# Attention stage of a two-layer trunk: one 384-column projection per unit from dense token copies

## The chip, the cores and the metric

The kernel runs on one core of one Trainium2 chip. The time is device microseconds of one execution; the kernel before took 3385.18 us (median of three runs, 3384.01 to 3385.2). TensorE (PE) multiplies, VectorE (DVE), ScalarE (ACT) and GpSimd (POOL) work element by element, and SyncE's queue (SP) issues DMAs. PEld is TensorE's weight load, which overlaps its matmuls.

## The reference

One sequence of 1024 tokens with 1024 channels goes through two layers. Layer 0 mixes tokens by attention, layer 1 by an mLSTM; each is followed by a squared-ReLU MLP. Only the attention is touched by the change:

```python
qkv = (x @ w_in).reshape(b, s, 3, N_GROUPS, ATTN_HEADS, ATTN_HEAD_DIM)   # 3 groups, 16 heads of 64
for g, (window, dilation) in enumerate(((128, 1), (512, 4), (2048, 16))):
    q = rms_norm(qkv[:, :, 0, g], q_gain[g]) * (ATTN_HEAD_DIM ** -0.5)
    k = rms_norm(qkv[:, :, 1, g], k_gain[g])
    o, l = dilated_window_attention(q, k, qkv[:, :, 2, g], rel_bias[:, g], window, dilation)
wts = softmax(stack(lses), axis=0)             # the three groups are merged by their denominators
y = einsum('gbsh,gbshe->bshe', wts, stack(outs))
x = x + y @ w_out
```

A query at token t sees the tokens t, t-d, ..., t-window of its group, where d is the group's dilation: 1, 4 or 16.

## The kernel before, in words

Every matrix product is made from two halves of each operand, hi and lo, in three matmuls: hi times hi, hi times lo, lo times hi (`split_matmul`, lines 67 to 71). A product over 1024 channels is thus 24 matmuls, 8 channel tiles by 3.

The attention stage (`attention_phase`) works on 24 sections: 8 pairs of heads by 3 groups, the group being the section number modulo 3. A section has 8 steps j, one for each 128 tokens, and a unit is one block of 128 queries of one section. All engines run the same list of steps (`run_supersteps`), and are held together by semaphores alone, each of them strictly in the order in which its own code is written. T counts the steps (8 times the superstep, plus j).

In step T TensorE does, in this order: query and key of the 128 tokens of step T (24 matmuls of 256 columns into ps_qk, with the tokens as the stationary operand); the transposes of the normed query and key of the step before, and of one block of values (ps_t); the transposes of probabilities (ps_p); a quarter of the values of half of the tokens (6 matmuls of 512 columns into ps_v, the weights stationary, the tokens streamed in their natural order); the scores of one unit (ps_s); and the product of probabilities and values of the unit before it (ps_o). Units run 8 steps behind the projection. A unit whose queries also see the block of keys before it has two blocks of keys (it is called two-block here) and takes twice the transposes and value products: 7 of 8 units in group 0, 4 of 8 in group 1 and none in group 2.

Where the group's dilation is not 1, ScalarE and VectorE reorder tokens after the fact: they read ps_t and ps_v in a strided order (`perm_view`) when they write qk_hi, qk_lo and vT.

ScalarE in step T: exponentials of a unit (L635), the copies of a finished output block out of ps_o (L651, L652), the hi half of the next section's weights (L602), the squares of query and key (L667), and what was transposed in this step (L673, L684, L688). The output copies of step T need the ps_o product of step T-1. VectorE: bias and row maximum of a unit (L723), the sums of squares (L732, L737), the lo halves (L743, L758, L764), the normed query and key (L779), and in some steps a piece of the merge of the three groups (L804 to L847; 1024 columns in the large ones). GpSimd: the lo half of the weights (L857), and a power of four numbers per token, rs (L879).

After the attention stage the projection of its output starts (the first matmul into first_ps), and then come the MLP, the mLSTM and the second MLP, none of which changes.

## Time and profile before

| | |
|---|---|
| median of three runs | 3385.18 us |
| the profiled execution's own time | 3383.74 us |
| its span, first to last instruction | 3382.0 us |
| TensorE busy | 3192.3 us (94%) |
| VectorE, ScalarE, GpSimd busy | 1334.0, 1102.1, 825.2 us |
| granted TensorE clock, mean | 0.978 |

Matmuls are pipelined, so their busy times overlap and the distance from one start to the next is what one costs. The same holds to a lesser degree on ScalarE and VectorE, where an instruction may start about 0.1 us before the one ahead of it has ended. The attention stage fills the first 1333 us of the span.

### The profile page before, as it was taken

What the parts mean: (1) busy time and instruction counts of PE and PEld (TensorE: products, weight loads), DVE (VectorE), ACT (ScalarE), POOL (GpSimd) and SP (SyncE); (2) the same over time, 40 slices, a digit from 0 to 9 for tenths busy, and PEclk for the clock granted to TensorE, in tenths of its full rate; (3) what the DMA queues carried; (4) which work ended last, traced back from release to release, by engine and by line L of the source; (5) the groups of instructions that cost most, each with busy time, mean ns of one, the idle gap of its engine ahead of it and who ended that gap; (6) DMA issues with size and microseconds to landing.
All of it is one profiled execution on the core that took longest, in us unless ns stands there. A gap on an engine that the chain in (4) does not pass through costs nothing. (4 is left out here: it accounts for less than half of the span.)

```text
span 3382.0 us, 48256 instructions
## 1 busy us (share of the span) xinstructions
PE 3192.3 (94%) x17466; PEld 2669.5 (79%) x17466; DVE 1334.0 (39%) x3725; ACT 1102.1 (33%) x3002; POOL 825.2 (24%) x598
## 2 busy tenths in 40 slices
PE   4999999999999995999999999899877999999999
PEld 3888888888888883878888888678655788888887
DVE  6445454555555554341313133541064431313131
ACT  4555555555555553321111112210244211111020
POOL 3332333333233320212222122112111122222221
PEclk9999999999999995999999999999998999999999
DMA  2112121211112114111111111111201111111112
GB/s 98 36 40 59 41 58 40 61 49 50 52 45 53 47 32 150 50 44 47 48 50 44 50 50 45 38 44 50 81 26 57 44 50 44 50 50 44 50 45 80
DMA packets 89904, 177.01 MB, mean 52 GB/s; under 512 B 25515, under 2 KB 55870, under 8 KB 89662
## 3 DMA queue, kind: packets, MB, share of 16 engines
q1 hardware_dynamic: 87358, 169.63, 16.1%
q10 hardware_dynamic: 2304, 4.20, 0.3%
q8 instruction: 147, 2.41, 0.3%
q14 instruction: 95, 0.78, 0.1%
HBM read 160.67 MB, written 13.12 MB: 51 GB/s over the span
## 5 line engine op out<-in xcount | busy, mean ns | idle before, releaser
L69 PE MATMUL ps_qk<-w_hi,attn_hT_hi 128*128 128x256 f32 x1536 | 437.4, 285 | 23.3 <-DVE attn_hT_lo L213 9.7
L915 POOL TENSOR_TENSOR first_w_lo<-first_raw,first_w_hi 128x1024 fp32r<-128x1024 f32 x96 | 231.7, 2414 | 900.8 <-ACT first_w_hi L911 900.8
L70 PE MATMUL ps_qk<-w_lo,attn_hT_hi 128*128 128x256 f32 x1536 | 436.1, 284 | 0.0
L71 PE MATMUL ps_qk<-w_hi,attn_hT_lo 128*128 128x256 f32 x1536 | 436.1, 284 | 0.0
L857 POOL TENSOR_TENSOR w_lo<-raw,w_hi 128x384 fp32r<-128x384 f32 x192 | 194.6, 1015 | 701.9 <-ACT w_hi L602 701.9
L915 POOL TENSOR_TENSOR second_w_lo<-second_raw,second_w_hi 128x1024 fp32r<-128x1024 f32 x72 | 172.2, 2391 | 630.0 <-ACT second_w_hi L911 630.0
L69 PEld LDWEIGHTS ps_qk<-w_hi,attn_hT_hi 128*128 128x128 f32 x1536 | 294.1, 191 | 27.6 <-issue 13.3
L635 ACT ACTIVATE prob<-ps_s,neg_max 128x128 f32<-128x128 f32 (+1 forms) x384 | 156.6, 413 | 439.7 <-DVE neg_max L726 439.7
L70 PEld LDWEIGHTS ps_qk<-w_lo,attn_hT_hi 128*128 128x128 f32 x1536 | 294.7, 192 | 0.4
L71 PEld LDWEIGHTS ps_qk<-w_hi,attn_hT_lo 128*128 128x128 f32 x1536 | 294.9, 192 | 0.0
L69 PE MATMUL first_ps<-first_hid_hi,first_w_hi 128*128 128x512 f32 x640 | 255.4, 399 | 32.7 <-DVE first_hid_lo L1239 32.7
L732 DVE TENSOR_REDUCE ss<-sq 128x4 f32<-128x256 f32 x192 | 80.7, 420 | 506.9 <-ACT sq L667 506.9
L69 PE MATMUL first_ps<-first_hT_hi,first_w_hi 128*128 128x512 f32 x640 | 252.6, 395 | 14.2 <-POOL first_w_lo L915 14.2
L69 PE MATMUL second_ps<-second_hid_hi,second_w_hi 128*128 128x512 f32 x640 | 251.0, 392 | 12.5 <-DVE second_hid_lo L1242 12.5
L70 PE MATMUL first_ps<-first_hid_lo,first_w_hi 128*128 128x512 f32 x640 | 254.9, 398 | 0.0
L71 PE MATMUL first_ps<-first_hid_hi,first_w_lo 128*128 128x512 f32 x640 | 254.7, 398 | 0.0
L70 PE MATMUL first_ps<-first_hT_lo,first_w_hi 128*128 128x512 f32 x640 | 251.4, 393 | 0.0
L71 PE MATMUL first_ps<-first_hT_hi,first_w_lo 128*128 128x512 f32 x640 | 251.4, 393 | 0.0
L70 PE MATMUL second_ps<-second_hid_lo,second_w_hi 128*128 128x512 f32 x640 | 250.5, 391 | 0.0
L71 PE MATMUL second_ps<-second_hid_hi,second_w_lo 128*128 128x512 f32 x640 | 250.1, 391 | 0.0
L879 POOL TENSOR_TENSOR rs<-var,minus_half 128x4 f32<-128x4 f32 x192 | 193.3, 1007 | 133.5 <-DVE var L737 125.0
L911 ACT CAST first_w_hi<-first_raw 128x1024 fp32r<-128x1024 f32 x96 | 99.9, 1041 | 383.6 <-PE first_ps L71 358.5
(276 smaller groups left out, 6853.9 us busy)
## 6 DMA issues: line engine op xcount, KB each, us to landing
raw<-in_wqkv SPq DMA_DIRECT2D x192, 192.0 KB, 2.3
first_raw<-in_w SPq DMA_DIRECT2D x64, 512.0 KB, 3.4
second_raw<-in_w SPq DMA_DIRECT2D x64, 512.0 KB, 3.4
w_bc<-share_dram SPq DMA_DIRECT2D x48, 256.0 KB, 4.2
first_raw<-in_vo_pieces SPq DMA_DIRECT2D x16, 512.0 KB, 3.5
bias<-bias_dram SPq DMA_DIRECT2D x16, 256.0 KB, 3.6
yT_dram<-o_g SPq DMA_DIRECT2D x8, 512.0 KB, 3.1
first_raw<-in_attn_wo SPq DMA_DIRECT2D x8, 512.0 KB, 3.5
```

The source lines that it names most:

```text
L69: pe.matmul(out, a_hi, b_hi, start=first, stop=False)
L70: pe.matmul(out, a_hi, b_lo, start=False, stop=False)
L71: return pe.matmul(out, a_lo, b_hi, start=False, stop=last)
L635: a = act.activation(prob[:, u % 2, h, c0:2 * P], ps_s[h][:, c0:2 * P], ACT.Exp, bias=neg_max[:, sp_, h * TT + u:h * TT + u + 1], accum_ou ...
L732: dve.tensor_reduce(ss[:], sq[:].rearrange("p (h e) -> p h e", e=HD), AX.X, ALU.add)\
L857: pool.tensor_tensor(w_lo[:, par, k, :], raw[:, slot, :], w_hi[:, par, k, :].bitcast(F32), ALU.subtract).then_inc(w_lo_done, 1)
L879: pool.tensor_tensor(rs[:], var[:], minus_half[:], ALU.pow).then_inc(rs_done, 1)
L911: act.copy(self.hi[:, n % 2, :], self.raw[:, n % self.RAW, :]).then_inc(self.hi_done, 1)
L915: pool.tensor_tensor(self.lo[:, n % 2, :], self.raw[:, n % self.RAW, :], self.hi[:, n % 2, :].bitcast(F32), ALU.subtract).then_inc(self.lo ...
```

## The change

The 128 tokens of a step are now the tokens of the unit itself, and not 128 neighbours. For group 1 these are tokens 4 apart, for group 2 tokens 8 apart (every second one of which belongs to another residue of the dilation 16, and is masked by the bias table). Query, key and value of the unit are then one product: 24 matmuls of 384 columns into ps_qkv, the unit's tokens stationary. The 6 matmuls of 512 columns, the tile vT, its copies by ScalarE and its transposes are gone.

For groups 1 and 2 the stationary operand is read from dense copies: ScalarE writes tile_hi, GpSimd writes tile_lo (128 partitions by 1024 columns each, two buffers), one step ahead. Group 0 reads the hidden state directly. In a step of TensorE the product with the values (ps_o) now stands directly behind the projection and works on a unit one step older than before; the scores are last. Units run 2 steps behind the projection, not 8. ScalarE still copies the output out of ps_o for the unit that is two behind its scores. The merge of the groups works on all 128 partitions with 8 columns in place of 64 with 16; its small pieces come one superstep earlier, and its five large ones (1024 columns each, L830 to L847 before) now stand in the steps j = 1, 3, 4, 5 and 6 of a section of group 1. Before, the first stood at j = 7 of such a section and the others at j = 1 to 4 of the next.

```diff
+def tile_view(h, section, u):
+
+    if section % NG == 1:
+        return h[:].rearrange("p k (n i r) -> p k r n i", n=2, r=4)[:, :, u // 2, u % 2, :]
+    return h[:].rearrange("p k (m u) -> p k u m", u=TT)[:, :, u, :]
...
-LAST_SUPER = SECTIONS + 2
+LAST_SUPER = SECTIONS + 1
+LAG = 2
...
-            return TT <= TT * st + j - back < TT * (SECTIONS + 1)
+            return 0 <= TT * st + j - LAG - back < TT * SECTIONS
 
         def unit(st, j, back):
 
-            sec, u = divmod(TT * (st - 1) + j - back, TT)
-            return sec, u
+            return divmod(TT * st + j - LAG - back, TT)
...
+        def next_tile(st, j):
+
+            st, j = (st, j + 1) if j + 1 < TT else (st + 1, 0)
+            return (st, j) if st < SECTIONS and st % NG else None
...
+                def project(k_first, k_end):
+
+                    g = st % NG
+                    for k in range(k_first, k_end):
                         if st == 0 and j % 4 == 0:
                             norm.wait_tile(pe, j // 4, k)
                         if j == 0:
                             pe.wait_ge(w_hi_done, TT * N + k + 1)
                             pe.wait_ge(w_lo_done, TT * N + k + 1)
-                        mm = split_matmul(pe, ps_qk[j % 2][:, 0:2 * P],
-                                          hT_hi[:, k, j * P:(j + 1) * P], hT_lo[:, k, j * P:(j + 1) * P],
-                                          w_hi[:, par, k, 0:2 * P], w_lo[:, par, k, 0:2 * P], k == 0, k == KT - 1)
-                    mm.then_inc(qk_mm, 1)
-                if (st >= 1 or j >= 1) and st <= SECTIONS:
-
+                        h_hi = tile_hi[:, j % 2, k, :] if g else hT_hi[:, k, j * P:(j + 1) * P]
+                        h_lo = tile_lo[:, j % 2, k, :] if g else hT_lo[:, k, j * P:(j + 1) * P]
+                        mm = split_matmul(pe, ps_qkv[j % 2][:, 0:W3], h_hi, h_lo,
+                                          w_hi[:, par, k, :], w_lo[:, par, k, :], k == 0, k == KT - 1)
+                    return mm
...
+                if st < SECTIONS:
+                    if st >= 1 or j >= 2:
+                        pe.wait_ge(qkn_done, T - 1)
+                        pe.wait_ge(v_lo_done, T - 1)
+                    if st % NG:
+                        pe.wait_ge(tile_hi_done, tiles_copied(i, st, j))
+                        pe.wait_ge(tile_lo_done, tiles_copied(i, st, j))
+                    project(0, KT).then_inc(qkv_mm, 1)
+                if has_unit(st, j, 2):
+
+                    sec, u = unit(st, j, 2)
+                    g = sec % NG
+                    pe.wait_ge(p_hi_done, U - 1)
+                    pe.wait_ge(p_lo_done, U - 1)
+                    pe.wait_ge(v_lo_done, U - 1)
+                    if has_unit(st, j, 3):
+                        pe.wait_ge(o_done, U - 2)
+                    first = 0 if has_prev(g, u) else 1
+                    for b in range(first, 2):
+                        slot = u - 1 + b
+                        mm = split_matmul(pe, ps_o[:, 0:2 * P], v_hi[:, slot, :], v_lo[:, slot, :],
+                                          pT_hi[:, b, :], pT_lo[:, b, :], b == first, b == 1)
+                    mm.then_inc(pv_done, 1)
...
-                    half = j // 4
-                    if j == 0 and st >= 1:
-                        pe.wait_ge(vT_done, 2 * N)
-                    if j == 4:
-                        pe.wait_ge(vT_done, 2 * N + 1)
-                    for k in range(2 * (j % 4), 2 * (j % 4) + 2):
-                        mm = split_matmul(pe, ps_v[:], w_hi[:, par, k, 2 * P:3 * P], w_lo[:, par, k, 2 * P:3 * P],
-                                          hT_hi[:, k, half * HALF:(half + 1) * HALF],
-                                          hT_lo[:, k, half * HALF:(half + 1) * HALF], k == 0, k == KT - 1)
-                    if j % 4 == 3:
-                        mm.then_inc(v_mm, 1)
...
+                ahead = next_tile(st, j)
+                if ahead is not None:
+                    act.wait_ge(qkv_mm, T)
+                    act.copy(tile_hi[:, (j + 1) % 2], tile_view(hT_hi, *ahead).bitcast(F32)).then_inc(tile_hi_done, 1)
                 if st < SECTIONS:
-                    act.wait_ge(qk_mm, T + 1)
+                    act.wait_ge(qkv_mm, T + 1)
                     if TT * st + j >= 1:
                         act.wait_ge(reduced, T)
-                    act.activation(sq[:], ps_qk[j % 2][:, 0:2 * P], ACT.Square).then_inc(squared, 1)
+                    act.activation(sq[:], ps_qkv[j % 2][:, 0:2 * P], ACT.Square).then_inc(squared, 1)
+                    act.copy(v_hi[:, j, :], ps_qkv[j % 2][:, 2 * P:W3]).then_inc(v_hi_done, 1)
...
+                    dve.tensor_tensor(v_lo[:, j, :], ps_qkv[j % 2][:, 2 * P:W3], v_hi[:, j, :].bitcast(F32), ALU.subtract)\
+                        .then_inc(v_lo_done, 1)
...
-                if st >= 4 and (st - 4) % NG == 0:
+                if st >= 3 and (st - 3) % NG == 0:
...
-                    if j == 7:
-
-                        o0 = o_raw[0][:, ((st - 4) // NG) % 2, :]
+                if st >= 4 and (st - 4) % NG == 0:
+                    pair = (st - 4) // NG + 2 * i
+                    o0 = o_raw[0][:, ((st - 4) // NG) % 2, :]
+                    if j == 1:
...
+                ahead = next_tile(st, j)
+                if ahead is not None:
+
+                    pool.tensor_copy(tile_lo[:, (j + 1) % 2], tile_view(hT_lo, *ahead).bitcast(F32)).then_inc(tile_lo_done, 1)
```

What stands on TensorE from the end of one projection to the scores, before (the unit is two-block; ident marks a transpose):

```order
L71 MATMUL ps_qk<-w_hi,attn_hT_lo 128x256
L526 MATMUL ps_t<-ident,qkn 128x128 [waits at_qkn_done,at_turn_lo,at_turn_hi]
L526 MATMUL ps_t<-ident,qkn 128x128
L530 MATMUL ps_t<-ident,vT 128x128 [waits at_vT_done]
L547 MATMUL ps_p<-ident,prob 128x128 [waits at_p_lo_done,at_p_hi_done,at_exp_done]
L547 MATMUL ps_p<-ident,prob 128x128 x3
L69 MATMUL ps_v<-attn_hT_hi,w_hi 128x512 [waits at_vT_done]
L70 MATMUL ps_v<-attn_hT_lo,w_hi 128x512
L71 MATMUL ps_v<-attn_hT_hi,w_lo 128x512
L69 MATMUL ps_v<-attn_hT_hi,w_hi 128x512
L70 MATMUL ps_v<-attn_hT_lo,w_hi 128x512
L71 MATMUL ps_v<-attn_hT_hi,w_lo 128x512
```

and now, at the same place in a section of group 1 (the value product is that of a one-block unit, the transposes of ps_p those of a two-block one):

```order
L75 MATMUL ps_qkv<-w_hi,tile_lo 128x384
L73 MATMUL ps_o<-pT_hi,v_hi 128x256 [waits at_v_lo_done,at_o_done,at_p_lo_done,at_p_hi_done]
L74 MATMUL ps_o<-pT_lo,v_hi 128x256
L75 MATMUL ps_o<-pT_hi,v_lo 128x256
L548 MATMUL ps_t<-ident,qkn 128x128 [waits at_qkn_done,at_turn_lo,at_turn_hi]
L548 MATMUL ps_t<-ident,qkn 128x128
L565 MATMUL ps_p<-ident,prob 128x128 [waits at_p_lo_done,at_p_hi_done,at_exp_done]
L565 MATMUL ps_p<-ident,prob 128x128 x3
L73 MATMUL ps_s<-qk_hi 128x128 [waits at_exp_done,at_turn_lo,at_turn_hi]
```

The value products moved from the end of the step to directly behind the projection, and the transpose of vT is gone. The end of the scores and the start of the next projection now:

```order
L73 MATMUL ps_s<-qk_hi 128x128
L74 MATMUL ps_s<-qk_lo,qk_hi 128x128
L75 MATMUL ps_s<-qk_hi,qk_lo 128x128
L73 MATMUL ps_qkv<-w_hi,tile_hi 128x384 [waits at_tile_hi_done,at_tile_lo_done,at_v_lo_done,at_qkn_done]
L74 MATMUL ps_qkv<-w_lo,tile_hi 128x384
```

The projection waits for both copies, at_tile_hi_done and at_tile_lo_done. On ScalarE, one step with one-block units before:

```order
L635 ACTIVATE prob,stat<-ps_s,neg_max 128x128 x2
L651 COPY o_g<-ps_o 64x128
L652 COPY o_g<-ps_o 64x128
L661 REGISTER_ALU
L602 CAST w_hi<-raw 128x384
L664 REGISTER_ALU
L667 ACTIVATE sq<-ps_qk 128x256
L673 CAST pT_hi<-ps_p 128x256
L684 ACTIVATE qk_hi<-ps_t,gains 128x128 x2
L688 CAST v_hi<-ps_t 128x128
```

and now:

```order
L616 ACTIVATE prob,stat<-ps_s,neg_max 128x128 x2
L632 COPY o_g<-ps_o 64x128
L633 COPY o_g<-ps_o 64x128
L591 CAST w_hi<-raw 128x384
L646 CAST tile_hi<-attn_hT_hi 128x1024
L648 REGISTER_ALU
L651 ACTIVATE sq<-ps_qkv 128x256
L652 CAST v_hi<-ps_qkv 128x128
L658 CAST pT_hi<-ps_p 128x256
L666 ACTIVATE qk_hi<-ps_t,gains 128x128 x2
```

The copy tile_hi of the next unit's tokens (L646) came in behind the output copies (L632, L633) and the weights' hi half (L591), and ahead of the squares; the cast of v_hi moved ahead of the transposed tiles.

## Rows read from the trace of the kernel before

**Rows 1.** Busy time by stretch: PE, PEld, DVE, ACT, POOL, then clock, DMA share, GB/s.

```profile
600.00:1000.00 400.00, 386.39 (x2876) 343.42 (x2874) 215.82 (x862) 214.68 (x764) 125.24 (x125) 1.00 0.18 50
1285.00:1310.00 25.00, 12.33 (x52) 8.28 (x52) 8.25 (x49) 8.95 (x41) 0.00 (x0) 0.50 0.11 28
2500.00:2540.00 40.00, 32.00 (x187) 26.72 (x187) 26.74 (x76) 25.54 (x73) 4.03 (x4) 1.00 0.17 54
```

**Rows 2.** Timeline of TensorE, one step: start, us, engine, line, op, out<-in.

```profile
801.78 0.28 PE L69 MATMUL ps_qk<-w_hi,attn_hT_hi 128*128 128x256 f32 x1
...
804.54 0.29 PE L71 MATMUL ps_qk<-w_hi,attn_hT_lo 128*128 128x256 f32 x1
...
804.66 0.38 PE L526 MATMUL ps_t<-ident,qkn 128*128 128x128 f32 x2
...
804.88 0.27 PE L530 MATMUL ps_t<-ident,vT 128*128 128x128 f32 x1
...
804.99 0.38 PE L547 MATMUL ps_p<-ident,prob 128*128 128x128 f32 x2
...
805.44 0.39 PE L70 MATMUL ps_v<-attn_hT_lo,w_hi 128*128 128x512 f32 x1
...
806.36 0.40 PE L71 MATMUL ps_v<-attn_hT_hi,w_lo 128*128 128x512 f32 x1
...
806.69 0.39 PE L69 MATMUL ps_s<-qk_hi 64*128 64x256 f32 x2
...
807.25 0.38 PE L69 MATMUL ps_o<-pT_hi,v_hi 128*128 128x256 f32 x1
...
807.71 0.28 PE L69 MATMUL ps_qk<-w_hi,attn_hT_hi 128*128 128x256 f32 x1
```

**Rows 3.** Timeline of ScalarE, same columns.

```profile
803.12 0.25 ACT L651 COPY total<-ps_o 64x128 f32<-64x128 f32 x1
...
803.67 0.51 ACT L602 CAST w_hi<-raw 128x384 fp32r<-128x384 f32 x1
804.86 0.38 ACT L667 ACTIVATE sq<-ps_qk 128x256 f32<-128x256 f32 x1 [0.68 <-PE ps_qk L71]
...
809.66 0.25 ACT L651 COPY total<-ps_o 64x128 f32<-64x128 f32 x1
```

**Rows 4.** Groups by line: busy us, mean ns | idle before, releaser.

```profile
L911 ACT CAST first_w_hi<-first_raw 128x1024 fp32r<-128x1024 f32 x96 | 99.9, 1041 | 383.6 <-PE first_ps L71 358.5 <-DMA first_raw<-in_attn_wo 24.7 <-ACT mi_sig L1186 0.5
L804 DVE TENSOR_TENSOR top<-compact 64x32 f32<-64x32 f32 x7 | 1.2, 177 | 0.0
L806 DVE TENSOR_TENSOR top<-top,compact 64x32 f32<-64x32 f32 x7 | 1.4, 205 | 0.2
L837 DVE TENSOR_TENSOR w_bc<-w_bc,total 128x1024 f32<-128x1024 f32 x7 | 14.1, 2015 | 0.0
L840 DVE TENSOR_TENSOR o_g<-o_g,w_bc 128x1024 f32<-128x1024 f32 x7 | 8.5, 1211 | 0.0
L915 POOL TENSOR_TENSOR first_w_lo<-first_raw,first_w_hi 128x1024 fp32r<-128x1024 f32 x96 | 231.7, 2414 | 900.8 <-ACT first_w_hi L911 900.8
```

**Rows 5.** One line's instructions: duration ns min/median/max, first and last start.

```profile
L684 ACT ACTIVATE qk_hi<-ps_t,gains x100: 361/372/385, 110.1 to 417.6; 128x128 fp32r<-128x128 f32 x100
```

**Rows 6.** Timelines: squares of steps 2, 8 and 191, last exp, next stage.

```profile
70.24 0.39 ACT L667 ACTIVATE sq<-ps_qk 128x256 f32<-128x256 f32 x1 [4.30 <-PE ps_qk L71]
...
97.15 0.39 ACT L667 ACTIVATE sq<-ps_qk 128x256 f32<-128x256 f32 x1 [1.88 <-PE ps_qk L71]
...
1265.30 0.38 ACT L667 ACTIVATE sq<-ps_qk 128x256 f32<-128x256 f32 x1 [1.25 <-PE ps_qk L71]
...
1300.39 0.37 DVE L794 COPY compact<-stat 64x32 f32<-64x32 f32 x2
...
1332.47 0.76 PE L69 MATMUL first_ps<-first_hid_hi,first_w_hi 128*128 128x512 f32 x1 [30.91 <-DVE first_hid_lo L1239]
```

**Rows 7.** Waits of 60 to 1240 us: us in total, times, longest.

```profile
PE ps_qk L69 <- issue: 6.0, 2, 3.0
```

More of the change, by code:

```diff
@@ L54, in bias_onehot @@
         band = window // dilation
+        mixed = dilation // UNIT_STRIDE[g]
         for x in range(BIAS_LEN):
-            step = x - (P - 1)
-            if step < 0 or step > band:
+            step, other = divmod(x - (P - 1), mixed)
+            if step < 0 or step > band or other:
                 out[g, REL_BUCKETS, x] = 1.0
@@ L327, in __init__ @@
         sb = lambda n, s: ctx.enter_context(nc.sbuf_tensor(n, s, F32))
-        self.vT = sb("vT", [P, 2, SEQ])
+        with ExitStack() as early:
+            self.x_first = early.enter_context(nc.sbuf_tensor("x_first", [P, 2, SEQ], F32))
+        self.tile_hi = ctx.enter_context(nc.sbuf_tensor("tile_hi", [P, 2, KT, P], F32R))
+        self.tile_lo = ctx.enter_context(nc.sbuf_tensor("tile_lo", [P, 2, KT, P], F32R))
         self.o_g0 = sb("o_g0", [P, 2, SEQ])
@@ L349, in attention_phase @@
         gains = sb("gains", [P, 2, NG])
-        qk_hi = sb("qk_hi", [P, 2, 2, SEQ], F32R)
-        qk_lo = sb("qk_lo", [P, 2, 2, SEQ], F32R)
-        v_hi = sb("v_hi", [P, 3, P], F32R)
-        v_lo = sb("v_lo", [P, 3, P], F32R)
+        qk_hi = sb("qk_hi", [P, 2, SEQ], F32R)
+        qk_lo = sb("qk_lo", [P, 2, SEQ], F32R)
+        v_hi = sb("v_hi", [P, TT, P], F32R)
+        v_lo = sb("v_lo", [P, TT, P], F32R)
         sq = sb("sq", [P, 2 * P])
@@ L366, in attention_phase @@
         stat_rows = sb("stat_rows", [4 * TT, P])
-        vT, w_bc, prob = buffers.vT, buffers.w_bc, buffers.prob
+        w_bc, prob = buffers.w_bc, buffers.prob
         o_raw = [buffers.o_g0, total[:].rearrange("p (o t) -> p o t", o=1), buffers.o_g2]
         ring = sb("ring", [P, HALF])
-        compact = sb("compact", [64, NG, 2, 2, 16])
-        top = sb("top", [64, 2, 16])
-        diff = sb("diff", [64, NG, 2, 16])
-        grown = sb("grown", [64, NG, 2, 16])
-        part = sb("part", [64, NG, 2, 16])
-        den = sb("den", [64, 2, 16])
-        share = sb("share", [64, NG, 2, 16])
-        ps_qk = [ps(f"ps_qk{i}", [P, HALF]) for i in range(2)]
-        ps_v = ps("ps_v", [P, HALF])
+        tile_hi, tile_lo = buffers.tile_hi, buffers.tile_lo
+        compact = sb("compact", [P, NG, 2, 2, TT])
+        top = sb("top", [P, 2, TT])
+        diff = sb("diff", [P, NG, 2, TT])
+        grown = sb("grown", [P, NG, 2, TT])
+        part = sb("part", [P, NG, 2, TT])
+        den = sb("den", [P, 2, TT])
+        share = sb("share", [P, NG, 2, TT])
+        ps_qkv = [ps(f"ps_qkv{i}", [P, HALF]) for i in range(2)]
         ps_t = ps("ps_t", [P, HALF])
@@ L429, in _, with load_bias @@
             sp.dma_start(gains[HD:P, 1, :], k_gain).then_inc(gains_in, 16)
+            def load_bias(g, pair):
+                base = (g * HEADS + 2 * pair) * BIAS_LEN
+                width = 2 * P if g < 2 else P
+                sp.dma_start(bias[g][:], bass.AP(bias_dram.tensor, base, [[1, P], [BIAS_LEN, 2], [1, width]]))\
+                    .then_inc(bias_in[g], 16)
+            load_bias(0, 0)
             for n in range(TT + 4):
@@ L575, in step @@
                         mm = split_matmul(pe, ps_s[h][:, c0:2 * P],
-                                          qk_hi[rows, sp_, 0, u * P:(u + 1) * P], qk_lo[rows, sp_, 0, u * P:(u + 1) * P],
-                                          qk_hi[rows, sp_, 1, k0:(u + 1) * P], qk_lo[rows, sp_, 1, k0:(u + 1) * P],
+                                          qk_hi[rows, 0, u * P:(u + 1) * P], qk_lo[rows, 0, u * P:(u + 1) * P],
+                                          qk_hi[rows, 1, k0:(u + 1) * P], qk_lo[rows, 1, k0:(u + 1) * P],
                                           True, True)
                     mm.then_inc(scored, 1)
-                if has_unit(st, j, 1):
-                    sec, u = unit(st, j, 1)
-                    g = sec % NG
-                    whole = TT * sec + u
-                    pe.wait_ge(p_hi_done, U)
-                    pe.wait_ge(p_lo_done, U)
-                    if has_unit(st, j, 2):
-                        pe.wait_ge(o_done, U - 1)
-                    first = 0 if has_prev(g, u) else 1
-                    for b in range(first, 2):
-                        slot = (whole - 1 + b) % 3
-                        mm = split_matmul(pe, ps_o[:, 0:2 * P], v_hi[:, slot, :], v_lo[:, slot, :],
-                                          pT_hi[:, b, :], pT_lo[:, b, :], b == first, b == 1)
-                    mm.then_inc(pv_done, 1)
             norm.sums(pe)
@@ L701, in _ @@
         def _(dve):
-            dve.memset(bias[2][64:P, :, 64:P], MASKED).then_inc(set_done, 1)
             dve.wait_ge(gains_in, 64)
```

237 lines of the change are left out of this document (86 added, 151 removed).

## The prediction

> **What bounds the kernel now.** I read the busy time by stretch first. In a steady stretch of the attention stage TensorE is busy 386 of 400 us at full clock, and every other engine under 55% [rows 1]. So TensorE's own queue bounds the stage, and a step costs what it has to start. The timeline of one step says how that adds up [rows 2]: the starts of the 24 matmuls of 256 columns run from 801.78 to 804.54, 0.120 us apart; four intervals of 512 columns take 0.92 us, 0.230 each; two transposes 0.22; the transpose of vT 0.11; the scores of a two-block unit 0.56. The whole step, from one projection to the next, is 5.93 us. Over the stage I take the squares of query and key as a clock, one per step [rows 6]: steps 8 to 191 lie 1168.2 us apart, 183 intervals of 6.38, which contain two stalls of some 3 us at the back edges of the loop [rows 7]; steps 2 to 8, which have no units yet, lie 4.48 apart. After the last projection come eight units with nothing to cover them: 35.1 us to the last merge, and 32.1 more until the next stage starts [rows 6].
>
> **The projection.** The columns streamed stay the same: 24 x 256 + 6 x 512 = 9216 = 24 x 384. The trace has no matmul of 384 columns at full clock in this stage. Bounds: 0.75 of the 512 row is 0.1725 us, 1.5 times the 256 row is 0.180. I take the middle of the two rows, 0.175, thus 4.20 us for 24; before it was 24 x 0.120 + 6 x 0.230 = 4.26, and some 0.2 us of changing over into and out of ps_v. With the vT transpose TensorE alone would have about 0.3 us less per step. Its queue would then hold: one-block 4.20 + 0.35 (three value matmuls) + 0.22 + 0.20 + 0.10 + 0.49 = 5.56 us, two-block 4.20 + 0.70 + 0.22 + 0.36 + 0.10 + 0.68 = 6.26.
>
> The Trainium skill (TensorE: Matmul & The Clock Gate, section Back-to-back issue gap) gives N / 2.4 + 2.5 ns for one start to the next, 162.5 ns at 384 columns. Its figure for 256 is 109 ns where rows 2 show 120, so the trace disagrees, and the measurement decides; by the page the sum below would be 192 x 24 x 12.5 ns = 58 us lower.
>
> **The new wait, on which everything turns.** In groups 1 and 2 projection T+1 needs tile_hi of T+1. ScalarE writes it in step T, and its queue is strictly in order: ahead of the copy stand the output copies, and these need the value product of step T, which TensorE starts only after projection T. Before, they needed the product of the step before, and nothing on TensorE waited for them soon. So projection, value product, output copies, weight copy and token copy now form one ring without slack:
> - projection 4.20; one-block value product to its end 0.23 + 0.30 = 0.53 (two-block 0.35 more, by the 0.12 spacing of 256 columns);
> - output copies 0.55 (803.12 to 803.67) [rows 3]; weight copy 0.41, its 0.51 less the 0.1 by which the next instruction starts early;
> - the token copy, d; and 0.10 for three hand-overs between engines (0.03 each in the rows).
>
> That is 5.79 + d for a one-block unit and 6.14 + d for two. Behind the value product TensorE has only transposes and scores to do, 1.0 to 1.4 us, while ScalarE needs 0.96 + d.
>
> **The price d.** The copy reads 1024 elements per partition, 16 bytes apart in group 1 and 32 in group 2, and writes them densely. No ScalarE row shows that. The dense copy of that size takes 1.04 us [rows 4]: the low end. On ScalarE a strided read out of PSUM costs nothing: qk_hi takes 361 to 385 ns whatever the group [rows 5]. But on VectorE strided reads out of SBUF do cost: L837, with one operand far-strided, takes 2015 ns where the dense L840 takes 1211, 0.79 ns more per element; and L806, whose third operand lies 16 bytes apart in group 1's view, takes 205 where L804 takes 177, 0.88 ns per element for 32 [rows 4]. The source here is SBUF, so I add what VectorE pays, 0.81 us: d = 1.85. High end: GpSimd's 2.41 us for two dense inputs of that size, the slowest row there is.
>
> **The sum.** One-block 7.64 us, two-block 7.99. Group 1: 4 x 7.64 + 4 x 7.99 = 62.5. Group 2: 7 x 7.64 and a last step of about 6.9, since group 0 needs no copy: 60.4. Group 0: no ring, TensorE's own 4 x 5.56 and 4 x 6.26, plus about 2.4 for small merge pieces and late exponentials: 49.7.
>
> VectorE becomes the second ring: from the squares to the next output copy the rows show 804.86 to 809.66, 4.80 us for a two-block unit [rows 3]; with 0.55 + 0.41 + d + 0.2 ahead of it that is 7.8, only 0.2 to 0.8 under the first ring. The five large merge pieces (two of 2.0 us, three of 1.2; together 7.6) stand in it, in group 1: less the slack, 4.5 us per pair.
>
> Steps 8 to 191: 8 x (62.5 + 60.4 + 4.5) - 4.5 (first pair has no merge) + 7 x 49.7 + 6 (back edges) - 7.6 (183 intervals, not 184) = 1361 against 1168: +193. Steps 2 to 8 carry units now, 5.8 in place of 4.48: +8. The tail shrinks: the last exponential comes three drain steps after the last projection, not eight; at about 3.4 us each with hand-over, some 11 us in place of 35: -24. The rest of the merge stays. Total +177 on the profiled execution's own 3383.7 (span 3382.0): 3561, and the median of the runs lies 1.4 above: **3562 us**.
>
> At nothing I cost: GpSimd's tile_lo, which starts when rs of the step before is done and has most of a step. GpSimd is busy 125 of 400 us, 2.0 per step [rows 1]; it would bind only above 5.5 us, and 2.41 x 2015 / 1211 is 4.0. The bias and compact DMAs, which SP issues at least a step ahead of use. VectorE's v_lo, which only moves its source.
>
> **The rivals.**
> - Strided reading is free on ScalarE (for it: rows 5; against it: they are PSUM). d = 1.04 takes 0.81 off 127 steps, 103 us, and the second ring gives back a little: 3462. Still slower, since 6.83 and 7.18 are above the old 6.38.
> - Only the 16-byte distance is free: group 2 pays, group 1 doesn't: 64 x 0.81 = 52 less, 3510. Against it: L806 pays at 16 bytes. The Trainium skill (SBUF — State Buffer, section Door 1: The DMA port swizzle) says lines are 16 bytes and that fp32 can be strided by up to 4 for free; by this group 1 would be free and group 2 not.
> - It is faster: the ring doesn't close, because the copy runs ahead of the value product in some way that I don't see, and TensorE's own 5.56 and 6.26 decide. With VectorE's round the sections are about 50, 52 and 47: 184 steps near 1135, so -33 + 8 - 24 = -49: 3336. It decides if ScalarE ends the copy within the 1.0 to 1.4 us of transposes and scores; the order of its queue speaks against it.
> - Worse: TensorE idles 2.1 of 7.64 us, 73% busy. At 80% busy the clock stays 1.00, at 49% it is 0.50 [rows 1]. If it fell in a third of the 128 steps, each projection would take 4 us more: 3730. GpSimd over 5.5 us leads the same way.
>
> **How the numbers follow.** The forecast (d from 1.6 to 2.1) 0.56; free strides 0.21; group 1 alone free 0.10; faster 0.07; clock, GpSimd or a d above 2.2, 0.06. The range 3440 to 3640 takes in both free cases with an error of 20 us and, above, d = 2.4 (+70). Faster by over 0.2% (what a measurement of this kernel can tell) 0.07, within 0.2% 0.01, slower 0.92.
>
> **What would show it.** In the changed profile: TensorE idle about 2 us before the first ps_qkv matmul in groups 1 and 2, released by ScalarE's tile_hi, about 240 us in all, and nearly none in group 0; tile_hi at 1.85 us; 384-column starts 0.175 us apart; ScalarE's output copies released by ps_o; steps of 7.6 and 8.0; last exponential some 11 us behind the last projection; clock at 1.00. I am wrong if tile_hi is written before the value product ends, or if that wait is released by GpSimd.

## The result, and the profile after

The changed kernel takes 3780.53 us (median of 4 runs, 3777.5 to 3787.34) against 3385.19 for the kernel before (4 runs, 3384.01 to 3388.77) on the same chip: ratio 1.1169, 95% interval 1.1149 to 1.1188. It is slower, as forecast, but by 395 us where 177 were forecast, and outside the range (3440 to 3640). The profiled execution has a span of 3779.4 us, 397.4 more than before, at a mean granted clock of 0.931 (before 0.978). An execution other than the profiled one shows the same clock within 0.003, so the profile stands for the runs.

The busy time by stretch, columns as in [rows 1]; the last three rows are single microseconds within one step:

```profile
600.00:1000.00 400.00, 326.25 (x1851) 307.16 (x1851) 188.18 (x655) 216.75 (x598) 157.25 (x125) 0.88 0.14 37
...
805.00:806.00 1.00, 0.48 (x2) 0.48 (x3) 0.09 (x1) 0.98 (x4) 0.00 (x0) 0.93 0.29 34
806.00:807.00 1.00, 1.00 (x4) 1.00 (x4) 0.94 (x3) 1.00 (x4) 0.39 (x1) 0.50 0.49 163
...
810.00:811.00 1.00, 1.00 (x7) 1.00 (x6) 0.00 (x0) 0.51 (x4) 0.00 (x0) 1.00 0.00 0
```

Two things differ from [rows 1]. TensorE is busy 326 of 400 us where it was 386, so it waits. And the clock, 1.00 before, is 0.88: within a step it stands at 0.50, the lower of the two levels (1.2 GHz), and comes back to 1.00. The timeline of TensorE over that step, columns as in [rows 2]:

```profile
801.43 0.34 PE L75 MATMUL ps_qkv<-w_hi,tile_lo 128*128 128x384 f32 x1
801.61 0.28 PE L73 MATMUL ps_o<-pT_hi,v_hi 128*128 128x256 f32 x1
...
803.48 0.28 PE L75 MATMUL ps_s<-qk_hi,qk_lo 64*128 64x128 f32 x2
805.52 0.44 PE L73 MATMUL ps_qkv<-w_hi,tile_hi 128*128 128x384 f32 x1 [1.76 <-ACT tile_hi L646]
...
806.06 0.53 PE L75 MATMUL ps_qkv<-w_hi,tile_lo 128*128 128x384 f32 x1
...
809.26 0.35 PE L73 MATMUL ps_qkv<-w_hi,tile_hi 128*128 128x384 f32 x1
809.45 0.33 PE L74 MATMUL ps_qkv<-w_lo,tile_hi 128*128 128x384 f32 x1
...
811.18 0.34 PE L75 MATMUL ps_qkv<-w_hi,tile_lo 128*128 128x384 f32 x1
```

After an idle stretch of 1.76 us the projection starts with the clock still at 0.93 on average (805 to 806), falls to starts 0.32 us apart from 806.06 to 809.26, and recovers to 0.173 (809.45 to 811.18, ten intervals). It lasts 5.8 us where 24 x 0.173 = 4.2 would do. Of the 128 projections from copies, 103 are slow like this one: they take 5.7 us from first to last start, the other 25 take 4.1. The same stretch on ScalarE, columns as in [rows 3], shows what held TensorE:

```profile
802.46 0.25 ACT L632 COPY total<-ps_o 64x128 f32<-64x128 f32 x1
...
803.01 0.51 ACT L591 CAST w_hi<-raw 128x384 fp32r<-128x384 f32 x1
803.43 2.04 ACT L646 CAST tile_hi<-attn_hT_hi 128x1024 fp32r<-128x1024 f32 x1
805.49 0.39 ACT L651 ACTIVATE sq<-ps_qkv 128x256 f32<-128x256 f32 x1
...
809.70 0.37 ACT L616 ACTIVATE prob<-ps_s,neg_max 128x128 f32<-128x128 f32 x1 [2.65 <-DVE neg_max L696]
```

Output copies, weight copy, token copy, then the projection 0.05 us behind it. Note that in this step the output copies do not wait for ps_o (its last product starts at 801.84); they stand behind the exponentials of 801.55 to 802.46, which waited for VectorE. Over steps 8 to 191 the first output copy waits for ps_o in 92 of 183 steps, 125 us in all; in the others something ahead of it in ScalarE's queue comes last. VectorE and GpSimd have this to show (start, us, engine, line, op):

```profile
738.81 2.52 DVE L788 TENSOR_TENSOR o_g<-o_g,w_bc 128x1024 f32<-128x1024 f32 x1
...
742.16 0.17 DVE L696 TENSOR_SCALAR neg_max<-stat 128x2 f32<-128x2 f32 x1
...
808.93 0.74 DVE L696 TENSOR_SCALAR neg_max<-stat 128x2 f32<-128x2 f32 x1
```

```profile
738.18 2.07 POOL L829 CAST tile_lo<-attn_hT_lo 128x1024 fp32r<-128x1024 f32 x1
...
807.57 2.06 POOL L829 CAST tile_lo<-attn_hT_lo 128x1024 fp32r<-128x1024 f32 x1
```

neg_max takes 0.17 us where GpSimd is quiet (742.16). At 808.93 it takes 0.74 and ends at 809.67; GpSimd's copy ends at 809.63. The merge piece at 738.81 ends at 741.33, which is the end of the copy (740.25) plus 1.08, about the piece's own 1.21 [rows 4]. So VectorE waits inside these instructions until GpSimd's copy is over, and no wait shows in the profile: only the duration grows. Of the 192 neg_max 84 take over 0.25 us, and each of them ends 0.025 to 0.037 us after a copy of GpSimd. e4 takes the copy away and settles it. The groups by line, columns as in [rows 4] (the second and the last two rows, x496 and x7, leave out what lies before 60 us and behind 1700):

```profile
L73 PE MATMUL ps_qkv<-w_hi,tile_hi 128*128 128x384 f32 x1024 | 428.0, 418 | 254.7 <-ACT tile_hi L646 240.3 <-issue 14.4
L73 PE MATMUL ps_qkv<-w_hi,attn_hT_hi 128*128 128x384 f32 x496 | 173.4, 350 | 0.0
L646 ACT CAST tile_hi<-attn_hT_hi 128x1024 fp32r<-128x1024 f32 x128 | 258.5, 2019 | 0.2
L829 POOL CAST tile_lo<-attn_hT_lo 128x1024 fp32r<-128x1024 f32 x128 | 264.4, 2065 | 0.0
L696 DVE TENSOR_SCALAR neg_max<-stat 128x2 f32<-128x2 f32 x192 | 78.2, 407 | 6.6
L792 DVE TENSOR_TENSOR w_bc<-w_bc,total 128x1024 f32<-128x1024 f32 x7 | 23.0, 3286 | 0.0
L788 DVE TENSOR_TENSOR o_g<-o_g,w_bc 128x1024 f32<-128x1024 f32 x7 | 17.5, 2493 | 0.0
```

The first two rows are the same matmul, from the copies (groups 1 and 2) and from the old layout (group 0): 418 ns against 350, the clock. 240.3 us of TensorE's idle time is released by tile_hi. The last two are two of the five merge pieces, a strided and a dense one, like L837 and L840 of [rows 4]: 3286 for 2015 and 2493 for 1211, both 1.3 us more.

The clock of steps, as in [rows 6]: squares of steps 2, 8 and 191, the last exponential, the next stage.

```profile
70.94 0.39 ACT L651 ACTIVATE sq<-ps_qkv 128x256 f32<-128x256 f32 x1 [4.82 <-PE ps_qkv L75]
...
112.00 0.38 ACT L651 ACTIVATE sq<-ps_qkv 128x256 f32<-128x256 f32 x1
...
1686.01 0.38 ACT L651 ACTIVATE sq<-ps_qkv 128x256 f32<-128x256 f32 x1
...
1697.09 0.36 ACT L616 ACTIVATE prob<-ps_s,neg_max 128x128 f32<-128x128 f32 x1
```

```profile
1731.11 0.76 PE L73 MATMUL first_ps<-first_hid_hi,first_w_hi 128*128 128x512 f32 x1 [30.88 <-DVE first_hid_lo L1198]
```

Steps 2 to 8 take 41.1 us (26.9 before): +14. Steps 8 to 191 take 1574.0 (1168.2): +406. From the last squares to the next stage 45.1 (67.2): -22. The sum is +398, the whole difference, so everything lies in this stage. The seventh to ninth sections, one of each group, take 57.5 us (group 0), 79.4 (group 1) and 67.8 (group 2), by the starts of the squares.

### The profile page after: what moved, and what is told of

Read it like the earlier page. It is cut to its first block and busy times, and to the rows that moved or that the text cites. A ratio compares the mean times of both kernels' runs of the same rounds, so it can differ in the third digit from the quotient of the medians.

```text
span 3779.4 us, 46141 instructions
## 1 busy us (share of the span) xinstructions
PE 3324.2 (88%) x16122; PEld 2859.6 (76%) x16122; DVE 1431.9 (38%) x3716; ACT 1325.5 (35%) x3082; POOL 1083.7 (29%) x726
## 5 line engine op out<-in xcount | busy, mean ns | idle before, releaser
L73 PE MATMUL ps_qkv<-w_hi,tile_hi 128*128 128x384 f32 x1024 | 428.0, 418 | 254.7 <-ACT tile_hi L646 240.3
L73 PEld LDWEIGHTS ps_qkv<-w_hi,tile_hi 128*128 128x128 f32 x1024 | 246.3, 241 | 275.1 <-ACT tile_hi L646 176.4
L74 PE MATMUL ps_qkv<-w_lo,tile_hi 128*128 128x384 f32 x1024 | 414.3, 405 | 0.0
L75 PE MATMUL ps_qkv<-w_hi,tile_lo 128*128 128x384 f32 x1024 | 412.2, 403 | 0.0
L829 POOL CAST tile_lo<-attn_hT_lo 128x1024 fp32r<-128x1024 f32 x128 | 264.4, 2065 | 0.0
L646 ACT CAST tile_hi<-attn_hT_hi 128x1024 fp32r<-128x1024 f32 x128 | 258.5, 2019 | 0.2
L74 PEld LDWEIGHTS ps_qkv<-w_lo,tile_hi 128*128 128x128 f32 x1024 | 246.8, 241 | 0.0
```

Of the source, the lines that this page charges most:

```text
L73: pe.matmul(out, a_hi, b_hi, start=first, stop=False)
L74: pe.matmul(out, a_hi, b_lo, start=False, stop=False)
L75: return pe.matmul(out, a_lo, b_hi, start=False, stop=last)
L646: act.copy(tile_hi[:, (j + 1) % 2], tile_view(hT_hi, *ahead).bitcast(F32)).then_inc(tile_hi_done, 1)
L829: pool.tensor_copy(tile_lo[:, (j + 1) % 2], tile_view(hT_lo, *ahead).bitcast(F32)).then_inc(tile_lo_done, 1)
```

## The experiments

Each is the changed kernel with the edit shown, timed in three rounds beside the kernel before; "step" is the distance of two squares.

**e1: the token copy first in ScalarE's step,** ahead of the exponentials.

```diff
+                ahead = next_tile(st, j)
+                if ahead is not None:
+                    act.wait_ge(qkv_mm, T)
+                    act.copy(tile_hi[:, (j + 1) % 2], tile_view(hT_hi, *ahead).bitcast(F32)).then_inc(tile_hi_done, 1)
...
                     hi_part(T, j % 4, (st + 1) % 2, j)
-                ahead = next_tile(st, j)
-                if ahead is not None:
-                    act.wait_ge(qkv_mm, T)
-                    act.copy(tile_hi[:, (j + 1) % 2], tile_view(hT_hi, *ahead).bitcast(F32)).then_inc(tile_hi_done, 1)
```

> ScalarE's token copy (tile_hi) stands first in its step, ahead of the exponentials and so ahead of the output copies that wait for the value product; nothing else changes. Theory A (the ring: TensorE waits for a copy that stands behind its own value product, and the idle time lets its clock fall): the idle time before ps_qkv goes from about 255 us to under 40, the granted clock of the attention stage from 0.88 to 0.99 or more, steps of groups 1 and 2 from 9.8 us to 6.0 to 6.6, and the whole time to 3330 to 3420 us. Theory B (the dense copies or the 384-column form disturb TensorE by themselves): the order on ScalarE changes little, the clock stays at 0.88 and the time above 3600 us.

Measured 3452.12 us (3446.82 to 3453.14), ratio 1.019 (1.0173 to 1.0207): 328 less than the changed kernel. Theory A holds in kind, and falls short in size: it allowed 3420 at most and a stage clock of 0.99, and the clock is 0.96 (600 to 1000 us). TensorE's wait for tile_hi is gone:

```profile
L73 PE MATMUL ps_qkv<-w_hi,tile_hi 128*128 128x384 f32 x1024 | 371.8, 363 | 6.6 <-DVE v_lo L740 6.6
...
L610 ACT CAST tile_hi<-attn_hT_hi 128x1024 fp32r<-128x1024 f32 x128 | 277.3, 2167 | 2.4 <-issue 2.4
```

The copy itself is no shorter (2167 ns). Its place in the queue is what made it cost. Most steps of group 2 are 6.2 to 6.5 us. The rest of the loss lies mostly in group 1, whose steps with merge pieces take 8.0 to 9.0 us; e5 goes after it.

**e2: extra matmuls in TensorE's wait.** 12 matmuls of 384 columns into a spare bank ahead of the wait for the copies, in groups 1 and 2; they compute nothing that is used. A wait for the section's first weights, which the extra matmuls read, was added with them.

```diff
                     if st % NG:
+                        for _ in range(12):
+                            pe.matmul(ps_fill[:, 0:W3], hT_hi[:, 0, 0:P], w_hi[:, par, 0, :], start=True, stop=True)
                         pe.wait_ge(tile_hi_done, tiles_copied(i, st, j))
```

> Before it waits for the token copies, TensorE runs 12 matmuls of 384 columns more per step of groups 1 and 2 into a spare bank (nobody reads it). Some 2.1 us, about as long as it idles. The ring stays closed. Theory A: the clock of the stage is 0.98 or more, the idle time falls to under 80 us, the projection takes 4.2 us again and steps 8.0 to 8.6 us; the whole time 3580 to 3660 us, faster by 120 to 200 us although 1536 matmuls are added. That prices the clock. Theory B (the clock falls or the matmuls are slow because of the copies, not the idle time): the clock stays near 0.88 and the time is 3780 us or above.

Measured 3706.95 us (3704.99 to 3713.85), ratio 1.0954 (1.0936 to 1.0973). The clock nearly did what was expected (0.97 for 0.98), the time did not: 74 less, where 120 to 200 were. The step is 8.15 us (one block) and 8.5, and in it TensorE no longer waits for tile_hi. ScalarE, VectorE and GpSimd over one step of group 2:

```profile
407.95 0.39 ACT L656 ACTIVATE sq<-ps_qkv 128x256 f32<-128x256 f32 x1
...
412.25 0.37 ACT L621 ACTIVATE prob<-ps_s,neg_max 128x128 f32<-128x128 f32 x1 [2.95 <-DVE neg_max L701]
...
413.91 2.18 ACT L651 CAST tile_hi<-attn_hT_hi 128x1024 fp32r<-128x1024 f32 x1
416.12 0.38 ACT L656 ACTIVATE sq<-ps_qkv 128x256 f32<-128x256 f32 x1
```

```profile
408.37 0.42 DVE L707 TENSOR_REDUCE ss<-sq 128x4 f32<-128x256 f32 x1 [4.30 <-ACT sq L656]
...
411.30 0.92 DVE L701 TENSOR_SCALAR neg_max<-stat 128x2 f32<-128x2 f32 x1
```

```profile
410.03 2.15 POOL L834 CAST tile_lo<-attn_hT_lo 128x1024 fp32r<-128x1024 f32 x1
```

This is a closed loop without TensorE: squares, VectorE's round, neg_max (0.92 us, held until GpSimd's copy ends at 412.18), exponentials, output copies, weight copy, token copy, squares: 8.17 us. It stands right behind the first ring, and takes over when the clock is given back. The 12 extra matmuls are themselves a little too many: with 8 of them and no copy on GpSimd the time is 18 us shorter than with 12 (e9 and e8). e4, e8, e9 and e10 take the rest apart.

**e3: dense reading.** Both copies read 128 neighbouring tokens, which are the wrong ones for groups 1 and 2; everything else stays.

```diff
-    if section % NG == 1:
-        return h[:].rearrange("p k (n i r) -> p k r n i", n=2, r=4)[:, :, u // 2, u % 2, :]
-    return h[:].rearrange("p k (m u) -> p k u m", u=TT)[:, :, u, :]
+    return h[:, :, u * P:(u + 1) * P]
```

> Both token copies read 128 neighbouring tokens in place of tokens 4 or 8 apart (the groups 1 and 2 then attend over the wrong tokens); same size and same place. Theory A: tile_hi goes from 2.02 to 1.04 us, tile_lo from 2.06 to some 1.2 us; the ring is 1.0 us shorter, 125 us in all, and since TensorE then idles only some 1.2 us per step the clock falls less often: 3560 to 3660 us. If the clock stops falling altogether, 3470 to 3520. Theory B: the time hardly moves, under 60 us.

Measured 3534.74 us (3521.66 to 3535.43), ratio 1.0427 (1.0405 to 1.045): 246 less than the changed kernel.

```profile
L73 PE MATMUL ps_qkv<-w_hi,tile_hi 128*128 128x384 f32 x1024 | 373.1, 364 | 136.4 <-ACT tile_hi L644 113.6 <-POOL w_lo L810 15.7 <-DVE v_lo L738 7.1
...
L827 POOL CAST tile_lo<-attn_hT_lo 128x1024 fp32r<-128x1024 f32 x128 | 133.2, 1041 | 0.0
L644 ACT CAST tile_hi<-attn_hT_hi 128x1024 fp32r<-128x1024 f32 x128 | 133.2, 1041 | 0.2
```

Both engines take 1041 ns for the dense copy and twice that for the strided one. The 0.98 us is worth 1.9 us per step, more than I expected. Three things shorten together, and this run doesn't tell their shares: the ring; GpSimd's hold on VectorE (neg_max is back at 170 ns, the merge pieces are 0.27 us longer than in [rows 4] and not 1.3); and TensorE's idle time, with which most of the low clock goes (21 slow projections for 103).

**e4: GpSimd's copy left out.** The products of the lo half read the neighbouring tokens.

```diff
-                        h_lo = tile_lo[:, j % 2, k, :] if g else hT_lo[:, k, j * P:(j + 1) * P]
+                        h_lo = hT_lo[:, k, j * P:(j + 1) * P]
...
-                        pe.wait_ge(tile_lo_done, tiles_copied(i, st, j))
...
-                    pool.tensor_copy(tile_lo[:, (j + 1) % 2], tile_view(hT_lo, *ahead).bitcast(F32)).then_inc(tile_lo_done, 1)
```

> GpSimd's token copy (tile_lo) is left out; the lo operand is read from the hidden state's neighbouring tokens (so the low halves of groups 1 and 2 are those of the wrong tokens). Theory A with VectorE's wait (neg_max, 0.17 us before, ended 0.04 us after GpSimd's copy in three of three places I read, 0.40 on average): neg_max is back to 0.17 us, and since VectorE's round lies beside ScalarE's ring and close to it, the time falls by 10 to 80 us: 3700 to 3770 us. Theory C (GpSimd's copy only looks like it holds VectorE): neg_max stays near 0.4 us and the time within 10 us of 3780.

Measured 3738.32 us (3736.96 to 3739.7), ratio 1.1039 (1.102 to 1.1057): 42 less, as expected. The wait for tile_hi is as long as it was, and neg_max and the merge pieces are free (L787 is L788 of the changed kernel, the first piece not counted):

```profile
L73 PE MATMUL ps_qkv<-w_hi,tile_hi 128*128 128x384 f32 x1024 | 417.6, 408 | 256.8 <-ACT tile_hi L645 241.9 <-issue 14.8
...
L695 DVE TENSOR_SCALAR neg_max<-stat 128x2 f32<-128x2 f32 x192 | 32.6, 170 | 6.5
...
L787 DVE TENSOR_TENSOR o_g<-o_g,w_bc 128x1024 f32<-128x1024 f32 x7 | 8.5, 1214 | 0.0
```

**e8: e2 and e4 together.** 12 extra matmuls, and no copy on GpSimd (the lo products read the neighbouring tokens).

> The 12 extra matmuls of e2 in groups 1 and 2, and GpSimd's copy of the lo halves left out (the products of the lo half read the neighbouring tokens). Theory A: with the clock restored, the step of e2 was set by the loop of ScalarE and VectorE, 8.15 us, in which neg_max was held for 0.75 us by GpSimd's copy. That 0.75 goes, and what is left is the first ring with the measured copy, 5.79 + 2.02 = 7.8 us one-block (TensorE's own queue with the extra matmuls, 5.56 + 2.09 = 7.65, lies just under) and 8.2 to 8.35 two-block. Sections 62.5 in group 2, 69 in group 1 with the merges; 3707 less 128 x 0.35 and some of the merges' lengthening: 3600 to 3660 us. Rival: the hold of VectorE isn't on the path once the clock is full, and the step is set by something else: same as e2, 3690 to 3710.

Measured 3645.89 us (3643.97 to 3647.41), ratio 1.0765 (1.0747 to 1.0783): 61 less than e2, and inside the 3600 to 3660 that theory A gave. The hold of VectorE is on the path once the clock is full. With the clock as it fell (e4) it was worth 42.

**e9: as e8, with 8 extra matmuls.** It was to leave only the ring that the prediction worked out.

> As e8, with 8 extra matmuls in place of 12: 1.39 us of them, so that TensorE's own queue is 6.95 us one-block and 7.65 two-block, and only the ring can set the step. It tests the sum of the prediction with the copy at its measured 2.02 us, the clock full and GpSimd's copy gone: 7.81 and 8.16 us, 3562 + 128 x 0.17 = 3584; allowed 3565 to 3620 us. Rival 1: the clock falls again with 8 (granted clock of the stage under 0.95): above 3650. Rival 2: VectorE's round without the hold, 7.8 us by the prediction's own count, is longer than that: 3620 to 3660.

Measured 3627.73 us (3623.86 to 3629.68), ratio 1.0711 (1.0693 to 1.0729): 8 above the allowed 3620, inside what rival 2 gave (3620 to 3660). One step of group 2 on ScalarE tells theory A from rival 2:

```profile
760.47 0.39 ACT L655 ACTIVATE sq<-ps_qkv 128x256 f32<-128x256 f32 x1
...
764.03 0.37 ACT L620 ACTIVATE prob<-ps_s,neg_max 128x128 f32<-128x128 f32 x1 [2.22 <-DVE neg_max L700]
...
765.42 0.26 ACT L636 COPY o_g<-ps_o 64x128 f32<-64x128 f32 x1 [0.59 <-PE ps_o L75]
...
765.98 0.51 ACT L595 CAST w_hi<-raw 128x384 fp32r<-128x384 f32 x1
766.40 2.15 ACT L650 CAST tile_hi<-attn_hT_hi 128x1024 fp32r<-128x1024 f32 x1
768.57 0.38 ACT L655 ACTIVATE sq<-ps_qkv 128x256 f32<-128x256 f32 x1
```

The output copies wait for ps_o, after the exponentials: here the first ring sets the step, 8.10 us. It is the prediction's ring with longer terms: from the projection to the first output copy 4.92 us (4.20 + 0.53 and a hand-over were summed), the two copies 0.56, the weights 0.42, the token copy 2.15 for 1.85. It isn't so everywhere: in 98 of 183 steps the output copies wait for ps_o, while in the steps of group 1 with the large strided merge pieces (9.7 us) they come straight behind exponentials that waited for VectorE. There rival 2 has a share.

**e10: the changed kernel with 8 extra matmuls, GpSimd's copy in place.**

> The changed kernel with 8 extra matmuls in groups 1 and 2 (e2 with 8 in place of 12), GpSimd's copy in place: the step between e9 and the changed kernel. Theory A: the clock stays near full as in e9 (0.98), and against e9 only the hold of VectorE by GpSimd's copy comes back, which cost 61 us between e8 and e2: 3628 + 61 = 3689, allowed 3670 to 3710 us; the step is 8.15 us one-block and 8.5 two-block by ScalarE's and VectorE's loop, as in e2, whatever the number of extra matmuls. Rival 1: TensorE idles more than in e9, since the loop is longer, and the clock falls again in part: 3710 to 3770, granted clock of the stage under 0.95. Rival 2: the 12 extra matmuls did not lengthen e2 at all, and the hold costs what is between e9 and e2: 3700 to 3715 at full clock.

Measured 3698.5 us (3696.43 to 3701.85), ratio 1.0927 (1.0908 to 1.0945), as theory A expected. Against e9 only the copy on GpSimd came back (with TensorE's reading of it): +71. Against the changed kernel only the extra matmuls did: -82.

```profile
600.00:1000.00 400.00, 362.36 (x2189) 334.05 (x2188) 196.13 (x681) 227.90 (x623) 166.33 (x131) 0.96 0.15 40
```

The seventh to ninth sections take 55.8 + 77.7 + 61.2 us here, 53.4 + 69.8 + 60.6 in e9. Most of GpSimd's price, some 50 of 71 us, lies in group 1, where the merge pieces are: a step with a strided piece grew from 9.7 to 10.9 us, a step of group 2, where only neg_max is held, from 8.03 to 8.13.

**e7: the lag of the values undone.** The value product goes back to the end of TensorE's step, one unit behind; the copies and the joint projection stay.

```diff
                     project(0, KT).then_inc(qkv_mm, 1)
-                if has_unit(st, j, 2):
...
-                    mm.then_inc(pv_done, 1)
...
+                if has_unit(st, j, 1):
+
+                    sec, u = unit(st, j, 1)
...
+                    mm.then_inc(pv_done, 1)
```

> The lag of the values alone is undone: TensorE's value product stands last in its step again and works on the unit one behind the scores; ScalarE's order is the changed kernel's, with the token copy behind the output copies. Theory A (the ring is the value product directly ahead of the output copies that the token copy stands behind): the output copies of a step need the product of the step before, the ring is open, TensorE doesn't wait for tile_hi, clock 0.96 or more, 3420 to 3480 us, like e1_copy_first. Rival: the place of the token copy behind the exponentials is enough to hold TensorE: waits for tile_hi stay above 100 us and the time above 3550 us.

Measured 3723.79 us (3720.28 to 3729.97), ratio 1.1006 (1.0988 to 1.1025). Theory A expected 3420 to 3480 and is wrong on this point; the rival's time (above 3550) came, but not its wait. The wait for tile_hi did go, and another of the same length came:

```profile
L73 PE MATMUL ps_o<-pT_hi,v_hi 128*128 128x256 f32 x280 | 101.5, 363 | 281.3 <-ACT pT_hi L658 247.4 <-issue 32.6 <-DVE pT_lo L713 1.0
```

pT_hi stands behind the token copy in ScalarE's queue as the squares do, so the value product now waits for it. The order of the value product is thus worth 57 of the 395 us; the rest stays with the copy in the middle of ScalarE's step, whichever product comes next.

**e5: the token copy first, and the squares early.** As e1, with the weight copy beside it and the squares and v_hi ahead of the output copies.

What is added here stands at the start of the step (the first three) and behind the exponentials (the last two), and is taken away from its old place.

```diff
+                    act.copy(tile_hi[:, (j + 1) % 2], tile_view(hT_hi, *ahead).bitcast(F32)).then_inc(tile_hi_done, 1)
+                if st + 1 < SECTIONS:
...
+                    hi_part(T, j % 4, (st + 1) % 2, j)
...
+                    act.activation(sq[:], ps_qkv[j % 2][:, 0:2 * P], ACT.Square).then_inc(squared, 1)
+                    act.copy(v_hi[:, j, :], ps_qkv[j % 2][:, 2 * P:W3]).then_inc(v_hi_done, 1)
```

> As e1_copy_first, and on ScalarE the weight copy comes early in the step and squares and v_hi stand ahead of the output copies, so the squares follow the projection at once and not behind value product and output copies. Theory D (what e1_copy_first still loses, 66 us on the kernel before, is VectorE's round from squares to exponentials, in which the large merge pieces stand): the round is some 1 us shorter, the merge steps of group 1 go from 8.0 to 9.0 us to 7.0 to 8.0, group 0's 8.5 us step shrinks, and the time is 3395 to 3430 us. Theory E (the merge pieces cost what they cost wherever the squares are): within 10 us of 3452.

Measured **3357.65 us** (3355.7 to 3358.76), ratio 0.9919 (0.9902 to 0.9935): faster than the kernel before by 0.8%, and better than the 3395 to 3430 that I expected. Steps of group 2 are down to 5.64 us:

```profile
803.46 0.38 ACT L634 ACTIVATE sq<-ps_qkv 128x256 f32<-128x256 f32 x1 [1.03 <-PE ps_qkv L75]
...
809.10 0.39 ACT L634 ACTIVATE sq<-ps_qkv 128x256 f32<-128x256 f32 x1 [0.93 <-PE ps_qkv L75]
```

ScalarE now waits for TensorE (1.03 us), not the other way round. TensorE's own queue was summed at 5.56 in the prediction.

**e6: e5, with GpSimd's copy behind neg_max.** GpSimd's copy moves behind the lo half of the weights; a small operation on GpSimd waits for the neg_max of the step, and the copy follows it.

```diff
+                    pool.wait_ge(neg_done, T - LAG)
+                    pool.tensor_tensor(held_back[:], minus_half[:], minus_half[:], ALU.subtract)
                     pool.tensor_copy(tile_lo[:, (j + 1) % 2], tile_view(hT_lo, *ahead).bitcast(F32)).then_inc(tile_lo_done, 1)
```

> As e5_early_squares, and GpSimd's token copy waits until VectorE's neg_max of the step is done (one more four-element instruction carries the wait). Theory D with VectorE held by the copy: neg_max is back to 0.17 us from 0.4 to 0.5; in the merge steps, where the round binds, this gives 0.3 to 0.6 us each, 10 to 40 us in all, so 3370 to 3415 us. If the later copy becomes what TensorE waits for, it is slower than e5_early_squares, and the wait before ps_qkv names tile_lo.

Measured 3356.39 us (3355.08 to 3356.74), ratio 0.9915 (0.9899 to 0.9932): the same as e5, where I expected a gain of 10 to 40 us or a loss. neg_max fell from 297 to 209 ns on average, and TensorE now waits 26.6 us for tile_lo. Group 1 gained 2 us per section (55.1 to 53.0), group 2 lost as much (46.6 to 49.0).

## Why the forecast held in sign and failed in size

- **The ring: right.** TensorE's idle time in front of the joint projection is 240.3 us, released by ScalarE's tile_hi, and none of it in group 0: "about 240 us in all, and nearly none in group 0". The other sign, output copies released by ps_o, came in only half of the steps. e1 shows it is the place of the copy that costs (328 us back). e7 shows that one link of the account was too narrow: I put the ring down to the output copies needing the value product of the same step. There are two rings of nearly one length through the same stretch of ScalarE, and the second, through exponentials, VectorE and squares, stays when the first is cut.
- **The projection: right.** Starts of 384 columns at full clock lie 0.173 apart (0.175 taken), at the lower of the two bounds from which it was taken (0.1725 and 0.180).
- **The copy: right in kind, 9% short in the end.** 2.02 us, in both groups (on average 2005 ns in group 1, 2033 in group 2), for 1.85; inside the 1.6 to 2.1 of the forecast, and both rivals with free strides are out. Over 128 steps +22 us. In e9 and e10, where TensorE idles less, it takes 2.17 to 2.18 us in group 2 and 2.03 to 2.04 in group 1; what lengthens it there was not tested. That VectorE's price per element foretold ScalarE's so nearly is partly luck: over the dense copy ScalarE pays 0.98 us, VectorE's rows gave 0.81.
- **"Group 0: no ring": wrong at its end, and a hit that is luck.** ScalarE makes the copy of group 1's first tile in the last step of group 0. By the squares of e9 the last two steps of group 0 take 9.14 and 8.26 us, the others 5.6 to 6.7, and the section 53.4 for 49.7. Group 2's section, 60.6 for 60.4, comes out right by two errors: six steps of 8.0 to 8.4 us and then 5.95 and 5.64, where seven of 7.64 and one of 6.9 were summed.
- **"GpSimd's tile_lo at nothing": wrong.** I asked only whether GpSimd would be done in time. It was (the projection never waited for it), but while it copies, VectorE's neg_max and merge pieces stand still. Price with the clock held near full: 71 us (e9 to e10); at the clock as it fell: 42 (e4). The Trainium skill (SBUF — State Buffer, section Who interferes with whom) says that a VectorE instruction with two SBUF inputs, or in a 2-port mode, is fully blocked while a GpSimd instruction that started first reads SBUF. The trace agrees for the merge pieces, which have two such inputs (2493 ns for 1211). neg_max has one; it is held all the same. That section of the Trainium skill counts tensor_scalar, its operation, among those that can run in such a mode; no run here tells whether it does. This is the rule that I should have weighed, and did not.
- **"Clock at 1.00": wrong, the largest term.** I gave 0.06 to a rival that shares its number with this mechanism, since 73% busy seemed nearer to the 80% at clock 1.00 than to the 49% at 0.50 [rows 1]. Both are means over 25 to 40 us, and say nothing of a pause of 1.8 us within a step: in the changed kernel TensorE is busy 326 of 400 us, 82%, and its clock is 0.88. The rival's price was nearly right by luck: it had a third of the 128 projections 4 us longer each, 170 us; the trace has 103 of them 1.6 us longer each, 167 us. Giving the clock back returned 82 us (e10) or 74 (e2) with GpSimd's copy in place, where the second ring stands right behind, and 111 without it (e4 to e9).
- **The second ring: too short.** Put at 0.2 to 0.8 us under the first, it was, with neg_max held for up to 0.8 us, level with it. The sum itself had no such room for a one-block step: the 7.8 was worked out from a two-block round, and lies above the 7.64 of the one-block ring. "Less the slack, 4.5 us per pair" for the merge pieces fails for the same reason: they are 1.3 us longer each, 6.4 a pair.
- **The start and the tail:** +14 for +8, and -22 for -24.

The sum in the order of the experiments: forecast 3562; 66 more for terms of the ring that were too short and for longer sections (e9, 3628; by its squares some 29 of them in group 0, 27 in group 1 with its merges, 1 in group 2, 8 at the start and the tail); 71 for VectorE held by GpSimd (e10, 3698.5); 82 for the clock: 3780.5. The shares of the last two depend on the order in which they are taken: the other way round it is 111 for the clock and 42 for GpSimd. So the steps of the prediction that failed are the clock at 1.00, GpSimd's copy at nothing, and the ring's terms. Not settled is why the clock falls in some steps and not in others: the projection from 797.37 to 801.61 ran at full clock behind a pause of 2.3 us, and the next, behind 1.8 us, did not. Over the stage the pause is 1.97 us on average ahead of a slow projection and 2.06 ahead of the others, so its length alone doesn't tell.

## What to carry to other kernels

A copy made one step ahead is only ahead if the queue that issues it lets it be: put it first in the step, and ask of each instruction behind it who waits for that. A wait of 2 us in every step of a matmul-bound loop is not priced by its length alone, because the clock of the matmuls behind it can fall; work out the step at both levels. Before an idle GpSimd is given a large copy from SBUF, look at what VectorE does in that time.
